# Token factors laid on by VectorE's evictions in an mLSTM and attention layer, with a changed prologue and gate block order

## The chip, the cores and the metric

The kernel runs on one core of a Trainium2 chip. The metric is the device time of one execution in microseconds; the kernel before takes 1875.45 us, the median of 3 runs (1875.11 to 1876.63). All times inside a profile count from the start of the span, and L-numbers are lines of the kernel before.

## What is computed

One decoder layer on x of 1024 tokens by 1024 features, all in float32:

```python
xn   = rms_norm(x, norm_mix_w)
proj = xn @ w_in        # da_q, da_k, da_v, ml_q, ml_k, ml_v, ml_i, ml_f, ml_o, gate_pre
oa   = diff_attention(rope(da_q), rope(da_k), da_v)       # 8 heads, q and k 2 x 64 wide, v 128
qk   = silu(causal_dwconv([ml_q, ml_k]))                  # 4 taps along the tokens
hm   = mlstm_chunkwise(qk[:512], qk[512:], ml_v, ml_i, ml_f)   # 8 heads
ob   = sigmoid(ml_o) * rms_norm(hm)
merged = sigmoid(gate_a) * (oa_normed @ w_proj_a) + sigmoid(gate_b) * (ob @ w_proj_b)
h    = x + merged @ w_out
h    = h + relu(rms_norm(h) @ w_ff1)**2 @ w_ff2
out  = rms_norm(h)
```

The root of the mean square of a token, by which `xn` divides, is one factor for each token. It commutes with the projection, so a projected row may be multiplied by it afterwards. Only that is used in what follows.

## The kernel before, in words

Each engine has its own instruction stream, written out by hand, and waits on semaphores; instructions of one engine run in order.

**Products.** Every float32 product is made of three on TensorE: each operand is split into a high part (a copy of ScalarE into a narrower type, `r1h`, `w_hi`) and a low part (the difference, `r1l`, `w_lo`, by VectorE or GpSimd). A weight block is 128 columns of the projection; a unit is one block for half of the tokens, 24 matmuls of 512 columns into one of the banks `gp[0]`, `gp[1]`. A unit is evicted to `ev[half]` and SP stores it in `proj_d`. `gp_free` counts evictions; TensorE waits before a unit for all but the latest one (L901).

**Blocks.** A head has HB = 6 blocks, 12 units: q (k = 0, 1), k (2, 3), the two values as token units (4 to 7, evicted with a factor of `rstd` for each token), the mLSTM's k and q (8, 9), and the output gate (10, 11). All of a head's units are evicted by ScalarE (`evac`, L1311). The rows of q and k get the token factors with cosT and sinT, which were multiplied by `roots` (L1849, L1850). The rows of blocks 4 and 5 are loaded back as `ckq` and `osig` and multiplied by `roots` on VectorE (L1965, L1978). After the heads come 16 gate blocks, whose units VectorE evicts with a product by `roots` (`gate_evac`, L1877).

**Rounds.** The units of head h+1 run beside the attention and mLSTM of head h (`attend`), in a round of 16 slots. QUARTERS says how many quarters of units TensorE makes in each slot: unit 8 in slot 10, unit 9 in 11, unit 10 in 12 and 13, unit 11 in 14. In a slot TensorE makes its quarters first and then its part of `attend`. The last head goes beside the gate blocks, 1.5 units a slot.

In a round VectorE ropes k and q in slot 0. In slot s = i + 3 it takes the maxima (`nb`) of score tile i, and after ScalarE's exponentials combines the two maps into `at` (L1953), which TensorE transposes in slot s = i + 4 (L1076) and ScalarE and VectorE split (`ath`, `atl`); the right part of a tile follows in slot i + 5 (`low(i, True)`, L1920). In slots 3 to 6 it also makes the convolution (`kqs`), in slot 14 the norm of the mLSTM output (`nd`), and in slot 15 the product into `osig` after TensorE's transposes (L1110).

**Prologue.** SP loads x in chunks of 2 k (`x_load`), weight block 0 after the second. ScalarE makes `r1h`, VectorE `r1l`. TensorE's `first_half` makes the input and forget gates and block 0, alternating every 4 k. ScalarE then squares eight token tiles (L1336) and takes the root (L1362), VectorE its reciprocal, TensorE spreads it by columns (`x_spread`, L940, after two quarters of unit 2) and ScalarE copies that to `roots`. Then ScalarE goes through the units k of head 0 with `prologue_step(k)` between them: exponential and logarithm for the gates (2), `tk` (7), Sin of the tables (8), `dc` (9). VectorE makes the tables beside it, and with `init_done` releases SP's loads of head 0.

**Order of queues.** SP's `head_round` sends the stores of two units, then a weight load, then the loads for `attend` (`att_loads`, L509; in the second round these come first after units 8 and 9). A weight load waits for the low part of the block two before it. ScalarE's and GpSimd's splits are in the same order.

```python
901:  wait(pe, gp_free, 2 * n + half - 1)
1312: wait(act, st[half], 16 * n)
1313: act.wait_ge(gemm_done, 2 * n + half + 1)
1398: for k in range(2 * HB):
1403:     evac(k // 2, k % 2, k - 4 if k // 2 in (2, 3) else None)
1404:     prologue_step(k)
```

Of the kernel before, what the change touches and what calls it, by code (L numbers as in the profile page):

```python
# [19 lines left out]
ALU = mybir.AluOpType  # L20
# [8 lines left out]
NH = 8  # L29
# [147 lines left out]
def build(nc, x, x_rows, x_halves, positions, in_blocks, in_if, columns, da_lambda,  # L177
# [12 lines left out]
    with ExitStack() as ctx:  # L190
# [230 lines left out]
        x_bc, roots_ready, o_scaled = sem("x_roots_spread"), sem("roots_ready"), sem("o_scaled")  # L421
# [39 lines left out]
        DVE_HEAD = 40  # L461
# [5 lines left out]
        def _(sp):  # L467
# [87 lines left out]
            sp.dma_start(wif[:].rearrange("p k n -> p (k n)"), in_if).then_inc(wif_in, 16)  # L555
            x_load(0, 1)
            wload_head(0, 0)
# [335 lines left out]
        def _(pe):  # L893
# [49 lines left out]
            def first_half(i):  # L943

                t = slice(i * HALF, (i + 1) * HALF)
                for part in range(2):
                    ks = range(4 * part, 4 * part + 4)
# [7 lines left out]
                    if part:  # L955
                        gates.then_inc(pro_pe, 1)
# [339 lines left out]
        def _(act):  # L1296
# [47 lines left out]
            for c in range(XC):  # L1344
# [7 lines left out]
                if c == 1:  # L1352
                    split_hi(0, 0, 0)
# [5 lines left out]
            for t in range(TT):  # L1359
                token_square(t)  # L1360
            act.wait_ge(x_sq, TT)
# [8 lines left out]
            def prologue_step(k):  # L1370
# [17 lines left out]
                if k == 8:  # L1388
# [4 lines left out]
                if k == 9:  # L1393
# [4 lines left out]
            for k in range(2 * HB):  # L1398
# [4 lines left out]
                evac(k // 2, k % 2, k - 4 if k // 2 in (2, 3) else None)  # L1403
                prologue_step(k)

            def attend(h, s, evac_units, splits=None, behind_k=None):
# [51 lines left out]
                if s == 7:  # L1458
                    act.wait_ge(conv_done, h + 1)
                    act.activation(sg[:], kqs[:], ACT.Sigmoid).then_inc(sg_ready, 1)  # L1460
                    act.wait_ge(o_scaled, h + 1)
# [28 lines left out]
            def head_round(h, att):  # L1490
                for s in range(SLOTS):
# [6 lines left out]
                    for k in ENDS_AT[s][:-1]:  # L1498
                        evac(h * HB + k // 2, k % 2, k - 4 if k // 2 in (2, 3) else None)

                    def evac_units():
                        for k in ENDS_AT[s][-1:]:
                            evac(h * HB + k // 2, k % 2, k - 4 if k // 2 in (2, 3) else None)
# [264 lines left out]
        def _(dve):  # L1768
# [18 lines left out]
            for i in range(2):  # L1787
                if i:
                    dve.wait_ge(x_in[XC], X_LOADED[XC])
                for k in range(KT):  # L1790
                    x_low(i, k)
                    if i == 0 and k == 3:
                        dve.wait_ge(w_hi, 1)
                        dve.tensor_tensor(wl[0][:], raw[0][:], wh[0][:].bitcast(F32), ALU.subtract).then_inc(w_split, 1)

# [51 lines left out]
            pro.link(dve.tensor_scalar(aw[:], aw[:], 1.0 - LAMBDA_INIT, None, ALU.mult))  # L1847
            dve.wait_ge(pro_act, 7)
            pro.link(dve.tensor_tensor(cosT[:], cosT[:], roots[:], ALU.mult))  # L1849
            pro.link(dve.tensor_tensor(sinT[:], sinT[:], roots[:], ALU.mult))  # L1850
            dve.wait_ge(c2_in, 16 * 2)
            dve.wait_ge(uw_st, 32)
            dve.sem_inc(init_done, 2)

# [22 lines left out]
            def gate_evac(k):  # L1877

                n, half = N_GATE + k // 2, k % 2
                dve.wait_ge(st[half], 16 * n)  # L1880
                dve.wait_ge(gemm_done, 2 * n + half + 1)
                if k == 0:
                    dve.wait_ge(gp_free, 2 * N_GATE)
# [757 lines left out]
```

## Time and profile before

| | |
|---|---|
| median of 3 runs | 1875.45 us (1875.11 to 1876.63) |
| profiled execution | 1879.1 us |
| its span | 1877.3 us, 26794 instructions |
| TensorE busy | 1848.6 us, 98% |
| VectorE, ScalarE, GpSimd busy | 1312.6, 972.0, 318.7 us |
| mean granted clock of TensorE | 0.995 of full |

The page is read from the top: the busy time of each engine shows which one can bound the kernel. Idle time of that engine is then looked up in its waits, where a row names the waiting engine, its tile and line, the releaser, and the sum, number and longest of the waits. A timeline row has start and duration in us, engine, line, operation, tiles and shapes; in brackets stands the idle time before it and what ended it. PEld is TensorE's weight load, SPq an issue on SP's queue.

### The profile page before, as it was taken

How to read it: one execution, taken by the hardware profiler on the slowest of the kernel's cores; microseconds unless marked ns; L12 is line 12 of the kernel's file. 1: busy time of each engine (PE TensorE's matmuls, PEld its weight loads, DVE VectorE, ACT ScalarE, POOL GpSimd, SP SyncE). 2: the span in 40 equal slices, each digit the busy share in tenths (PEclk: the TensorE clock that was granted, in tenths of full speed). 3: DMA queues.
4: the chain of work that ended last, by engine and by line, in shares of the span. 5: the costliest groups of instructions: out<-in, count | busy, mean ns of one | idle time of the engine just before them, and what ended most of it. 6: DMA issues, size and time to landing. Idle time of an engine off the chain costs nothing.

```text
span 1877.3 us, 26794 instructions
## 1 busy us (share of the span) xinstructions
PE 1848.6 (98%) x9698; PEld 1585.2 (84%) x9698; DVE 1312.6 (70%) x1705; ACT 972.0 (52%) x1565; POOL 318.7 (17%) x189
## 2 busy tenths in 40 slices
PE   8999999999999999999999999999999999999998
PEld 6989898989898989888878887878888888888887
DVE  6575858586767767666436867687868778688774
ACT  6355655656565656534214553237676585333343
POOL 2102020211111121244420313520000000021002
PEclk9999999999999999999999999999999999999999
DMA  7342515151424242365457735647768587464412
GB/s 284 96 159 69 179 57 196 50 188 60 159 79 162 84 162 89 133 208 183 146 211 266 257 110 195 219 161 265 243 228 294 192 280 264 157 232 150 154 71 90
DMA packets 112594, 318.34 MB, mean 170 GB/s; under 512 B 11496, under 2 KB 28520, under 8 KB 99456
## 3 DMA queue, kind: packets, MB, share of 16 engines
q1 hardware_dynamic: 110208, 308.86, 47.1%
q10 hardware_dynamic: 2304, 8.39, 1.1%
q8 instruction: 52, 0.85, 0.2%
q14 instruction: 30, 0.25, 0.0%
HBM read 221.71 MB, written 95.49 MB: 169 GB/s over the span
## 4 chain that ended last, share of the span: by engine, by line
PE 85%; DVE 8%; issue 3%; ACT 2%; DMA 1%; SPq 1%; DVEq 0%; POOL 0%; ACTq 0%
PE gp L904 7%; PE gp L906 7%; PE gp L905 7%; PE scores L1206 6%; PE scores L1210 6%; PE scores L1208 6%; PE gp L922 3%; PE gp L924 3%; PE gp L923 3%; PE gp L1206 2%; PE gp L1210 2%; PE gp L1208 2%; PE ob L1062 2%; PE ob L1063 2%; PE scores L1015 2%
## 5 line engine op out<-in xcount | busy, mean ns | idle before, releaser
L904 PE MATMUL gp<-r1h,w_hi 128*128 128x512 f32 x752 | 299.0, 398 | 7.6 <-ACT ev L1320 5.3
L906 PE MATMUL gp<-r1h,w_lo 128*128 128x512 f32 x752 | 295.7, 393 | 0.0
L905 PE MATMUL gp<-r1l,w_hi 128*128 128x512 f32 x752 | 294.8, 392 | 0.0
L1206 PE MATMUL scores<-fxh,fqh 128*128 128x512 f32 x512 | 199.8, 390 | 1.8 <-DVE fxl L2226 1.7
L1210 PE MATMUL scores<-fxh,fql 128*128 128x512 f32 x512 | 199.2, 389 | 0.0
L1208 PE MATMUL scores<-fxl,fqh 128*128 128x512 f32 x512 | 199.2, 389 | 0.0
L904 PEld LDWEIGHTS gp<-r1h,w_hi 128*128 128x128 f32 x752 | 142.4, 189 | 37.1 <-issue 3.4
L906 PEld LDWEIGHTS gp<-r1h,w_lo 128*128 128x128 f32 x752 | 142.1, 189 | 30.6
L905 PEld LDWEIGHTS gp<-r1l,w_hi 128*128 128x128 f32 x752 | 142.4, 189 | 27.8
L2452 POOL TENSOR_TENSOR w_lo<-w_raw,w_hi 128x1024 fp32r<-128x1024 f32 x25 | 60.5, 2421 | 501.7 <-ACT w_hi L1309 486.6
L924 PE MATMUL gp<-w_hi_pair,r1l 128*128 128x256 f32 x512 | 144.8, 283 | 0.0
L922 PE MATMUL gp<-w_hi_pair,r1h 128*128 128x256 f32 x512 | 144.8, 283 | 0.0
L923 PE MATMUL gp<-w_lo_pair,r1h 128*128 128x256 f32 x512 | 144.8, 283 | 0.0
L1449 ACT ACTIVATE pr<-scores,nb 128x256 f32<-128x256 f32 (+7 forms) x128 | 94.2, 739 | 77.3 <-DVE nb L1940 76.7
L2233 DVE TENSOR_TENSOR fxl<-xraw,fxh 128x2048 fp32r<-128x2048 f32 x54 | 123.3, 2283 | 0.0
L1629 ACT ACTIVATE fqh<-rq 128x2048 fp32r<-128x2048 f32 x32 | 61.2, 1913 | 106.2 <-DVE rq L2262 65.2
L1206 PEld LDWEIGHTS scores<-fxh,fqh 128*128 128x128 f32 x512 | 96.1, 188 | 22.6 <-DVE fxl L2226 2.1
L1208 PEld LDWEIGHTS scores<-fxl,fqh 128*128 128x128 f32 x512 | 96.1, 188 | 20.1 <-issue 0.2
L1210 PEld LDWEIGHTS scores<-fxh,fql 128*128 128x128 f32 x512 | 96.1, 188 | 20.0
L1641 ACT ACTIVATE fxh<-xraw 128x2048 fp32r<-128x2048 f32 x54 | 102.7, 1902 | 6.1 <-DMA xraw<-xo_d 6.1
L2237 DVE TENSOR_TENSOR fql<-rq,fqh 128x2048 fp32r<-128x2048 f32 x32 | 73.2, 2287 | 43.0 <-ACT fqh L1629 43.0
L923 PEld LDWEIGHTS gp<-w_lo_pair,r1h 128*128 128x128 f32 x512 | 97.4, 190 | 0.4
(426 smaller groups left out, 4536.2 us busy)
## 6 DMA issues: line engine op xcount, KB each, us to landing
xraw<-xo_d SPq DMA_DIRECT2D x62, 1024.0 KB, 4.8
w_raw<-in_in_blocks SPq DMA_DIRECT2D x64, 512.0 KB, 3.7
proj_d<-ev SPq DMA_DIRECT2D x128, 256.0 KB, 2.3
rq<-in_ff_quarters SPq DMA_DIRECT2D x32, 1024.0 KB, 7.6
xo_d<-res SPq DMA_DIRECT2D x78, 256.0 KB, 3.3
xo_d<-ring SPq DMA_DIRECT2D x60, 256.0 KB, 3.2
xo_d<-item SPq DMA_DIRECT2D x24, 256.0 KB, 2.5
pq<-in_sq_quarters SPq DMA_DIRECT2D x5, 1024.0 KB, 7.1
```

What stands on the lines that cost most here:

```text
L904: pe.matmul(gp[half][:], wh[slot][:, k, :], hi[:, k, t], start=(k == 0), stop=False)
L905: pe.matmul(gp[half][:], wh[slot][:, k, :], lo[:, k, t], start=False, stop=False)
L906: mm = pe.matmul(gp[half][:], wl[slot][:, k, :], hi[:, k, t], start=False, stop=(k == KT - 1))
L922: pe.matmul(to, r1h[:, kk, t], whp[:, kk].rearrange("p a n -> p (a n)"), start=(kk == 0), stop=False)
L923: pe.matmul(to, r1h[:, kk, t], wlp[:, kk].rearrange("p a n -> p (a n)"), start=False, stop=False)
L924: mm = pe.matmul(to, r1l[:, kk, t], whp[:, kk].rearrange("p a n -> p (a n)"), start=False, stop=(kk == KT - 1))
L1206: pe.matmul(bank, qh[s % 3][:, k, cols], xh[s % 3][:, k, :], start=first and k == 0, stop=False, skip_group_check=True)
L1208: pe.matmul(bank, qh[s % 3][:, k, cols], xl[s % 3][:, k, :], start=False, stop=False, skip_group_check=True)
L1210: mm = pe.matmul(bank, ql[s % 3][:, k, cols], xh[s % 3][:, k, :], start=False, stop=(k == UN - 1), skip_group_check=True)
L1449: act.activation(pr[:, c, 0:(i + 1) * P], sp_[:, c, 0:(i + 1) * P], ACT.Exp, bias=nb[:, c:c + 1], scale=-1.0, accum_out=rs[:, i, c:c + 1]) ...
L1641: act.activation(xh[s % 3][:], xraw[(s + 1) % 2][:], ACT.Copy).then_inc(p_hi, 1)
L2233: dve.tensor_tensor(xl[s % 3][:], xraw[(s + 1) % 2][:], xh[s % 3][:].bitcast(F32), ALU.subtract).then_inc(p_lo, 1)
```

## The change

It has six parts.

1. `scaled_evac` on VectorE evicts a unit with a product by `roots`; `head_evac` uses it for units 8 to 11 of every head, and `gate_evac` for the gate blocks. ScalarE skips these units. Where the evicting engine changes, the later one waits for the earlier one's count (k == 8 on VectorE, k == 0 on ScalarE).
2. The products by `roots` on `ckq` and `osig` are gone, with the semaphore `o_scaled`.
3. In a round `head_evac` stands before VectorE's part of `attend`, in slot 14 behind it. In the last round the gate evictions of slot 14 stand behind `attend` too.
4. In the prologue SP issues weight block 0 before the second chunk of x; ScalarE splits it after the first chunk and VectorE after two `r1l`; TensorE alternates every 2 k.
5. ScalarE evicts unit 0 behind the second token square.
6. Sin stands at step 7 of the prologue and `dc` at step 8. VectorE evicts units 8 to 11 of head 0 around the products of cosT and sinT, units 10 and 11 after it has signalled `init_done`.

```diff
             x_load(0, 0)
             sp.dma_start(cols[:], columns).then_inc(cols_in, 16)
             sp.dma_start(wif[:].rearrange("p k n -> p (k n)"), in_if).then_inc(wif_in, 16)
+            wload_head(0, 0)
             x_load(0, 1)
-            wload_head(0, 0)
...
-                for part in range(2):
-                    ks = range(4 * part, 4 * part + 4)
+                for part in range(4):
+                    ks = range(2 * part, 2 * part + 2)
...
                 x_high(0, 2 * c + 1)
-                if c == 1:
+                if c == 0:
                     split_hi(0, 0, 0)
...
             for t in range(TT):
                 token_square(t)
+                if t == 1:
+                    evac(0, 0)
...
-                if k == 8:
 
                     for i, tab in enumerate((sinT, cosT)):
...
-                if k == 9:
+                if k == 8:
                     act.wait_ge(pro_pe, 4)
...
-                evac(k // 2, k % 2, k - 4 if k // 2 in (2, 3) else None)
+                if 0 < k < 8:
+                    evac(k // 2, k % 2, k - 4 if k // 2 in (2, 3) else None)
...
-                    act.wait_ge(o_scaled, h + 1)
+                    act.wait_ge(o_in, 16 * h + 16)
...
                     def evac_units():
                         for k in ENDS_AT[s][-1:]:
-                            evac(h * HB + k // 2, k % 2, k - 4 if k // 2 in (2, 3) else None)
+                            if k == 0:
+                                act.wait_ge(gp_free, 2 * (h * HB))
+                            if k < 8:
+                                evac(h * HB + k // 2, k % 2, k - 4 if k // 2 in (2, 3) else None)
...
                     x_low(i, k)
-                    if i == 0 and k == 3:
+                    if i == 0 and k == 1:
...
+            def scaled_evac(n, half, behind=None):
+
+                dve.wait_ge(st[half], 16 * n)
+                dve.wait_ge(gemm_done, 2 * n + half + 1)
+                if behind is not None:
+                    dve.wait_ge(gp_free, behind)
+                dve.tensor_tensor(ev[half][:], gp[half][:], roots[:, half * HALF:(half + 1) * HALF], ALU.mult).then_inc(gp_free, 1)
+                dve.wait_ge(gp_free, 2 * n + half + 1)
+                dve.sem_inc(ev_ready[half], 1)
+
+            def head_evac(h, k):
+
+                n = h * HB + k // 2
+                scaled_evac(n, k % 2, 2 * n if k == 8 else None)
...
+            head_evac(0, 8)
             dve.wait_ge(pro_act, 7)
             pro.link(dve.tensor_tensor(cosT[:], cosT[:], roots[:], ALU.mult))
             pro.link(dve.tensor_tensor(sinT[:], sinT[:], roots[:], ALU.mult))
+            head_evac(0, 9)
             dve.wait_ge(c2_in, 16 * 2)
             dve.wait_ge(uw_st, 32)
             dve.sem_inc(init_done, 2)
+            head_evac(0, 10)
+            head_evac(0, 11)
...
+            def attend_round(h, s):
+
+                ends = [k for k in ENDS_AT[s] if k >= 8]
+                if s == SLOTS - 2:
+                    attend(h, s)
+                for k in ends:
+                    head_evac(h + 1, k)
+                if s != SLOTS - 2:
+                    attend(h, s)
...
-                    chain.link(dve.tensor_tensor(ckq[:, CONV - 1:], ckq[:, CONV - 1:], roots[:], ALU.mult))
...
-                        dve.wait_ge(o_in, 16 * h + 16)
-                        dve.tensor_tensor(osig[:], osig[:], roots[:], ALU.mult).then_inc(o_scaled, 1)
...
             for s in range(SLOTS):
+                if s == SLOTS - 2:
+                    attend(NH - 1, s, lows=False)
                 for k in GATE_UNITS_AT[s]:
                     if k > 2:
                         gate_evac(k)
-                attend(NH - 1, s, lows=False)
+                if s != SLOTS - 2:
+                    attend(NH - 1, s, lows=False)
```

## Rows read from the trace of the kernel before

**Rows 1.** The page, part 1: busy time, share of the span, instructions.

```profile
PE 1848.6 (98%) x9698; PEld 1585.2 (84%) x9698; DVE 1312.6 (70%) x1705; ACT 972.0 (52%) x1565; POOL 318.7 (17%) x189
```

**Rows 2.** Waits of TensorE: sum, number, longest, in us.

```profile
PE tr L1076 <- DVE at L1953: 7.2, 7, 1.1
PE gp L904 <- ACT ev L1320: 5.3, 2, 3.0
...
PE gp L904 <- POOL w_lo L2446: 2.3, 1, 2.3
```

**Rows 3.** Windows: one microsecond after the first stop of TensorE.

```profile
35.00:36.00 1.00, 1.00 (x4) 0.81 (x3) 0.00 (x0) 0.95 (x2) 0.37 (x1) 0.50 0.97 367
```

**Rows 4.** Timeline of the first 12 us, SP, ScalarE and TensorE.

```profile
2.13 0.43 SPq L550 DMA_DIRECT2D xt<-in_x_halves  x1
...
2.60 0.43 SPq L479 DMA_DIRECT2D w_raw<-in_in_blocks  x1
...
6.83 1.33 ACT L1340 ACTIVATE r1h<-xt,cols 128x512 fp32r<-128x512 f32 x2 [0.37 <-DMA xt<-in_x_halves]
...
8.88 1.06 ACT L1301 ACTIVATE w_hi<-w_raw 128x1024 fp32r<-128x1024 f32 x1 [0.71 <-DMA w_raw<-in_in_blocks]
...
11.25 0.19 PEld L960 LDWEIGHTS gp<-r1h,w_hi 128*128 128x128 f32 x1 [0.43 <-DVE w_lo L1794]
```

**Rows 5.** Timeline of ScalarE at the end of the token squares.

```profile
32.87 0.30 ACT L1362 ACTIVATE rstd<-ss,eps 128x8 f32<-128x8 f32 x1
33.08 1.30 ACT L1320 ACTIVATE ev<-gp 128x512 f32<-128x512 f32 x2
```

**Rows 6.** Timeline of TensorE around its first stop.

```profile
30.42 0.39 PE L962 MATMUL gp<-r1h,w_lo 128*128 128x512 f32 x1
33.80 0.47 PE L904 MATMUL gp<-r1h,w_hi 128*128 128x512 f32 x1 [2.99 <-ACT ev L1320]
...
38.21 1.05 PE L940 MATMUL tr<-ident,rstd 128*128 128x128 f32 x8
```

**Rows 7.** Timelines of VectorE, SP and ScalarE, 84 to 113 us.

```profile
84.61 1.23 DVE L1849 TENSOR_TENSOR cosT<-cosT,roots 128x1024 f32<-128x1024 f32 x1 [13.85 <-ACT dc L1395]
85.87 3.30 DVE L1850 TENSOR_TENSOR sinT<-sinT,roots 128x1024 f32<-128x1024 f32 x1
...
89.29 0.34 SPq L517 DMA_DIRECT2D kraw<-proj_d  x1
...
94.68 1.56 SPq L495 DMA_DIRECT2D proj_d<-ev  x2
...
102.48 0.60 ACT L1320 ACTIVATE ev<-gp 128x512 f32<-128x512 f32 x1 [4.68 <-DMA proj_d<-ev]
...
112.33 0.58 ACT L1320 ACTIVATE ev<-gp 128x512 f32<-128x512 f32 x1
```

**Rows 8.** Two lines of VectorE: min, median, max ns of one.

```profile
L1965 DVE TENSOR_TENSOR ckq<-ckq,roots x8: 1217/1219/1219, 120.0 to 825.7; 128x1024 f32<-128x1024 f32 x8
...
L1884 DVE TENSOR_TENSOR ev<-gp,roots x32: 677/691/692, 796.1 to 1001.0; 128x512 f32<-128x512 f32 x32
```

**Rows 9.** Timelines of VectorE and TensorE in slots 3 to 5 of a head.

```profile
317.41 1.22 DVE L1965 TENSOR_TENSOR ckq<-ckq,roots 128x1024 f32<-128x1024 f32 x1
...
322.64 0.44 PE L1076 MATMUL tr<-ident,at 128*128 128x128 f32 x2 [1.13 <-DVE at L1953]
```

**Rows 10.** Timeline of VectorE in slot 10.

```profile
361.45 0.42 DVE L1920 TENSOR_TENSOR atl<-tr,ath 128x256 fp32r<-128x256 f32 x1 [0.72 <-ACT ath L1426]
```

**Rows 11.** Timelines of VectorE, ScalarE and TensorE, slots 14 and 15 of the last round.

```profile
946.42 0.69 DVE L1884 TENSOR_TENSOR ev<-gp,roots 128x512 f32<-128x512 f32 x1 [4.75 <-PE gp L906]
...
951.97 1.06 ACT L1301 ACTIVATE w_hi<-w_raw 128x1024 fp32r<-128x1024 f32 x1 [0.49 <-PE gp L906]
...
955.50 0.52 PE L904 MATMUL gp<-r1h,w_hi 128*128 128x512 f32 x1 [2.34 <-POOL w_lo L2446]
```

**Rows 12.** Timeline of VectorE in slot 6 of the last round.

```profile
853.86 0.69 DVE L1884 TENSOR_TENSOR ev<-gp,roots 128x512 f32<-128x512 f32 x1 [5.60 <-DMA proj_d<-ev]
```

More of the change, by code:

```diff
@@ L420, in build @@
         x_sq, tok_in, x_std, x_rstd = (sem(n) for n in ("x_squared", "fourth_tokens_in", "x_std", "x_rstd"))
-        x_bc, roots_ready, o_scaled = sem("x_roots_spread"), sem("roots_ready"), sem("o_scaled")
+        x_bc, roots_ready = sem("x_roots_spread"), sem("roots_ready")
         x_hi, x_lo = sem("x_hi"), sem("x_lo")
@@ L459, in build @@
         ft_tr, ft_out, ft_act, out_st = sem("ft_tr"), sem("ft_out"), sem("ft_act"), [sem("out_st0"), sem("out_st1")]
-        DVE_HEAD = 40
+        DVE_HEAD = 39
         block = ctx.enter_context(nc.Block())
@@ L954, in first_half @@
                         gates = pe.matmul(sbank[:, i, :], wifl[:, k, :], r1h[:, k, t], start=False, stop=(k == KT - 1))
-                    if part:
+                    if part == 3:
                         gates.then_inc(pro_pe, 1)
@@ L1498, in head_round @@
                     for k in ENDS_AT[s][:-1]:
-                        evac(h * HB + k // 2, k % 2, k - 4 if k // 2 in (2, 3) else None)
+                        if k < 8:
+                            evac(h * HB + k // 2, k % 2, k - 4 if k // 2 in (2, 3) else None)
                     def evac_units():
                         for k in ENDS_AT[s][-1:]:
-                            evac(h * HB + k // 2, k % 2, k - 4 if k // 2 in (2, 3) else None)
+                            if k == 0:
+                                act.wait_ge(gp_free, 2 * (h * HB))
+                            if k < 8:
+                                evac(h * HB + k // 2, k % 2, k - 4 if k // 2 in (2, 3) else None)
                     attend(att, s, evac_units, splits if s >= 9 else None)
@@ L1877, in gate_evac @@
             def gate_evac(k):
[L1879 to L1883, printed above, removed]
-                dve.tensor_tensor(ev[half][:], gp[half][:], roots[:, half * HALF:(half + 1) * HALF], ALU.mult).then_inc(gp_free, 1)
-                dve.wait_ge(gp_free, 2 * n + half + 1)
-                dve.sem_inc(ev_ready[half], 1)
+                scaled_evac(N_GATE + k // 2, k % 2, None if k else 2 * N_GATE)
+            def attend_round(h, s):
[6 more added lines that the diff above has]
+                    attend(h, s)
             def attend(h, s, lows=True):
@@ L2037, in _ @@
             for s in range(SLOTS):
-                attend(0, s)
+                attend_round(0, s)
             with dve.Fori(1, NH - 1) as h:
                 for s in range(SLOTS):
-                    attend(h, s)
+                    attend_round(h, s)
             for s in range(SLOTS):
+                if s == SLOTS - 2:
+                    attend(NH - 1, s, lows=False)
                 for k in GATE_UNITS_AT[s]:
```

## The prediction

> **What bounds the kernel now.** I read the page first: TensorE is busy for 98% of the span [rows 1]. So only two things can shorten this kernel: fewer products on TensorE, of which the change removes none, or less idle time and less slow clock on it. Next came the waits of TensorE alone [rows 2]: seven waits of some 1.1 us on `at` of VectorE (one in each of seven heads, 7.2 us together), two on an eviction of ScalarE (5.3 us), one on a weight split of GpSimd (2.3 us). Others have no part in the change. Third, the clock [rows 3]: after the long idle stretches the granted clock falls from 2.4 to 1.2 GHz. In the first stretch, until 37.7 us, matmuls start 0.43 us apart in place of 0.228; the twelve from 33.80 to 38.21 [rows 6] take 4.4 us for 12 x 0.228 = 2.7, so the slow stretch costs 1.7. The same follows the idle times of 2.3 us before 112.96 and before 955.50; the idle times of 1.1 us are followed by none. Last, for each wait, the timelines of the other engines, to see who was late and why.
>
> **Start.** SP now issues weight block 0 (at 2.13 us) before the second chunk of x (2.60); ScalarE splits it after the first chunk, VectorE takes its low part after two `r1l`, and TensorE alternates gates and block every 2 k instead of 4. Today the second chunk, issued at 2.13, is there at 6.8, and block 0, issued at 2.60, at 8.9 [rows 4]. If the two landings swap, the high part is ready at 6.85 + 1.06 = 7.9, the low part at 7.95 + 1.22 = 9.2, and TensorE, after its first six gate products, asks for it at about 9.7. The second chunk at 8.9 gives `r1l` of k=2 at 10.3; TensorE wants it at 11.1. No wait is left, and the one on the split [rows 4], with the slow first matmul behind it, goes: 0.25 us. Bounds: nothing gained if the landings keep their times in other order, and a loss (third rival).
>
> **First eviction.** Today both evictions of block 0 stand behind eight token squares and the root, at 33.08 us, though the half-0 unit was done at 19.8. TensorE stops at 30.8 and goes on at 33.80 [rows 5, 6]. The change puts `evac(0, 0)` behind the second square, at about 25.2. It pushes six squares and the root by 0.6 + 0.1: the root lands at 33.9, its reciprocal on VectorE at 34.2. TensorE now begins unit 2 at 30.65, does 12 products (2.75 us), and at 33.4 meets the next late thing, the reciprocal that `x_spread` reads: 0.85 us idle, less than the 1.1 that leaves the clock up. `x_spread` (1.7) and 12 more products end at 38.75; today they end at 39.92 + 2.73 = 42.65. Gain 3.9, of which I take 3.8. Bound below: with the slow clock after 0.85 us all the same, 2.1.
>
> **Second wait on an eviction (110.6 to 112.96).** Its chain [rows 7]: `dc` and the two tables arrive late (Sin stands at step 8, `dc` at step 9), so cosT and sinT are multiplied at 84.61 to 89.2; that releases the loads of head 0 (89.29); SP issues twelve of them and a weight load before the store of unit 10 (94.68), which needs some 7.7 us; ScalarE waits for it until 102.48, then makes seven copies in order, and its next eviction is at 112.33. The change moves Sin to step 7 and `dc` to step 8 and leaves units 8 to 11 to VectorE. With the clock of the first term (TensorE 3.9 earlier): Sin ends near 73.2, the split of block 5 moves behind it (ScalarE 74.2, GpSimd 76.7, wanted by TensorE at 79), `dc` at 74.5, the two table products end by 77.1, or by 79.2 if they stretch as `sinT` did. VectorE then waits for unit 9 (79.4), evicts it, and releases the loads at 80.3, about 4.9 us earlier against TensorE than today. The store of unit 10 goes out near 86 and has 9 us. What VectorE now has in front of its rope work: the evictions of units 10 and 11, so that this begins at 91.1, 1.3 us later against TensorE. ScalarE evicts (head 1, unit 0) when TensorE has made it (95.9), reads `kraw` at 96.6 (roped at 94.9), and its next eviction ends at 106.4; TensorE wants it at 106.8. The wait of 2.29 and its slow stretch of 1.7 go: 4.0. The margin is 0.4 us.
> Here a rule can be weighed. The two table products ran 1.23 and 3.30 us [rows 7], the second beside a GpSimd split of 2.40. The Trainium skill, SBUF — State Buffer, section Who interferes with whom, says that a VectorE instruction with two SBUF inputs and a GpSimd one that reads SBUF exclude each other for a whole instruction. The trace agrees. By the rule the products, now beside the split of block 5, end at 79.2, without it at 77.1; both are before unit 9 is done, so the term is 4.0 by either, and only the chance of the second rival is larger with it.
>
> **Heads.** Removed for each head: `ckq` x `roots` and `osig` x `roots`, 1.22 us each, eight times [rows 8], on VectorE. Added: four evictions of 0.69 us on VectorE [rows 8]; removed: four of some 0.6 on ScalarE. VectorE's sum rises by 4 x 0.69 - 2.44 = 0.3 us a head, but the place counts. The product on `ckq` (317.41) stands between `at` of tile 0 and `at` of tile 1, and TensorE idles 1.13 us for the latter, from 321.5 [rows 9]. Without it all that follows on VectorE comes at least 1.22 earlier: `at` ends at 321.3. That leaves 0.1 to 0.2 us of margin. What is late next is nothing in this round with an idle row. The evictions stand where VectorE waits on TensorE anyway: units 8 and 9 at the head of slots 10 and 11, before `low(i, second)`. Added waits: on `gemm_done`, on the store of the buffer, and once a head on ScalarE's eviction of unit 7. For slot 10: `at` ends at 360.73, unit 7 is evicted at 360.86, the new one runs to 361.65, and `atl` ends at 362.1 instead of 361.87; TensorE asks for it at 362.64 [rows 10]. Unit 10 falls into free time in slot 13; unit 11 delays `osig` by 0.15 us in slot 15, which 0.5 us of idle before `ka` absorbs. Cover of 0.5 us, then; if it is gone, each of the four costs TensorE up to 0.69. Term: of 7.2 us I take 6.9. Bounds: 0 and 7.2.
>
> **Last round.** In slot 14 VectorE waits for units 21 and 22 before it starts on `nd` of the last head, though ScalarE had brought that at 935.7. So `nd` is done at 952.0, ScalarE stands behind its root until 950.1, splits the next weight at 951.97, GpSimd its low part until 955.45, and TensorE idles 0.32 and 2.34 us, with 1.7 of slow clock [rows 11]. With `attend` first, `nd` takes 935.8 to 940.5, before unit 21 is done (940.9), the split follows at 941 and GpSimd's at 944.5; TensorE wants it at 952.7. Gain 0.3 + 2.3 + 1.7 = 4.3. What is late next is nothing: the front's first loads wait for the store of `ob` as before and are wanted 20 us later.
>
> **Sum.** 0.25 + 3.8 + 4.0 + 6.9 + 4.3 = 19.2 us of 1879.1, the profiled execution (span 1877.3 and 1.8 around it): 1859.9. The median of the timed runs is 3.65 below that execution; with the same terms it becomes 1875.45 - 19.2 = 1856.2.
>
> **Rivals.**
> 1. The heads keep their wait: the chain from the eviction of unit 0 to `at` of tile 1 is tight, the margin 0.1 us, and one more late item in slot 5, 10 or 11 takes it back. For: the margins; against: every duration in that chain repeats within 0.01 us. Gain 12 to 13, 1863.
> 2. The wait at 110.6 stays, since VectorE's queue now holds two evictions before its rope work and the margin is 0.4 us. Gain 15.2, 1860.2.
> 3. Block 0 still lands at 8.9 or later: TensorE then stops at 9.7 for the low part until 11.3 (8.9 + 1.06 + 1.22), 1.6 us, with ScalarE's second chunk queued behind the split, and perhaps a slow stretch of 1.7. Gain 15.6 to 17.5, about 1859. The Trainium skill, DMA: Bandwidth & Descriptors, section Queues, rings and completion order, says that transfers issued in order need not complete in order; the landings here came in order of issue.
> 4. Slower: in slot 10 VectorE waits for the store of unit 6 before it may evict unit 8, and `low` and all of slot 10 stand behind it. One such wait of 5.6 us is in the trace, in the last round [rows 12], where TensorE did not stop. Beyond 0.8 us of cover TensorE would idle 4.8 us and get 1.7 of slow clock, 6.5 x 7 heads = 45, net 26 slower: 1902. It decides from 3.5 us of wait per head on. Against: in the round that I read, the store of unit 6 is issued at 349.6, 11 us ahead.
> 5. The idle time goes, but comes back at a later point that does not move, so that nothing is seen: 1875. Against: no wait behind 1000 us hangs on the start.
>
> **How the numbers follow.** Forecast 0.60 (1853 to 1859 by its own bounds), rival 1: 0.15, rival 2: 0.09, rival 3: 0.07, rival 4: 0.04, rival 5: 0.03, mixtures of the first three 0.02. Low end 1852.5: all terms full, a further wait of 0.9 us in the last head gone, and some 3 us for the distance between profiled and timed runs. High end 1865: rival 1, or 2 and 3 together. A change of 0.2% (3.75 us) is what a measurement of this kernel can tell; all of the first four cases are beyond it. Faster 0.93, same 0.03, slower 0.04.
>
> **What would show it.** Waits of TensorE: no row `tr <- at` of 1.1 us; no row on ScalarE's `ev` of 3.0 or 2.3; none on GpSimd's `w_lo` of 2.3; a new one before `tr<-ident,rstd` of under 1 us. The granted clock is full from 7 us until the turn near 1150. TensorE's time per head round falls from 98.8 to 97.7 us. `kraw` of head 0 is loaded at about 81. I am wrong if TensorE waits for `atl` or a `gp` bank in slots 5 or 10 to 14, if VectorE waits for a store there, or if a half-rate stretch appears before 38 us.

## The result, and the profile after

The kernel after takes 1857.61 us, the median of 4 runs (1856.95 to 1859.87), against 1876.04 for the kernel before (4 runs): a ratio of 0.9898, 95% interval 0.9883 to 0.9912. The profiled execution took 1859.87 us, its span is 1858.1; that is 19.2 us less than the profiled execution of before. The forecast was 19.2 less, 1859.9 for a profiled execution and 1856.2 for the median. Line numbers of after differ from those of before: L1808 is VectorE's `scaled_evac`, L1981 writes `at`, L1948 `atl`, L2218 `res`.

The page, part 1, to be held against [rows 1]:

```profile
PE 1843.9 (99%) x9698; PEld 1581.4 (85%) x9698; DVE 1314.7 (71%) x1721; ACT 952.7 (51%) x1533; POOL 317.8 (17%) x189
```

TensorE has the same 9698 matmuls, 4.7 us less busy time (less of it at 1.2 GHz) and 14.5 us less outside it. The waits of TensorE say which idle time went, against [rows 2]:

```profile
PE scores L931 <- POOL wifl L2483: 2.6, 1, 2.6
PE gp L1168 <- DVE res L2218: 2.2, 1, 2.2
PE scores L1206 <- DVE fxl L2254: 1.7, 1, 1.7
PE ob L1062 <- DVE atl L1948: 0.9, 1, 0.9
PE gp L904 <- DVE ev L1808: 0.5, 1, 0.5
```

All seven waits on `at`, both on ScalarE's `ev` and the one on `w_lo` are gone; one of 0.5 us on VectorE's eviction is new. A sum of waits does not show the clock, though. So I paired every matmul of after with its partner in before and followed the difference of their starts. It changes at few places:

| place (time in before) | difference before and behind it | in the forecast |
|---|---|---|
| start, up to unit 2 (30.65) | 0 to +0.27 | -0.25 |
| first eviction (30.8 to 37.4) | +0.27 to -4.42 | -3.8 |
| second wait on an eviction (112.96 to 117) | -4.33 to -8.33 | -4.0 |
| heads, seven waits on `at` | -8.33 to -15.64 | -6.9 |
| gate unit 3 (805.87) | -15.64 to -15.14 | none |
| last round (952 to 959) | -15.14 to -19.80 | -4.3 |
| front and rest | -19.80 to -19.26 | none |

A negative difference means that after is ahead. The last row is no part of the change as far as the runs show: the half microsecond arises between 960 and 1100 us, and in the run start_undone below, whose code is the same as after's there, the difference stays at -19.78 to -19.79.

**First eviction.** The timelines of ScalarE, VectorE and TensorE of after around 24 to 36 us, against [rows 5, 6]:

```profile
24.57 0.58 ACT L1320 ACTIVATE ev<-gp 128x512 f32<-128x512 f32 x1
...
33.21 0.30 ACT L1364 ACTIVATE rstd<-ss,eps 128x8 f32<-128x8 f32 x1
...
33.54 0.20 DVE L1839 RECIPROCAL rstd<-rstd 128x8 f32<-128x8 f32 x1
...
33.42 0.39 PE L906 MATMUL gp<-r1h,w_lo 128*128 128x512 f32 x1
33.80 1.16 PE L940 MATMUL tr<-ident,rstd 128*128 128x128 f32 x8
...
35.61 0.47 PE L904 MATMUL gp<-r1h,w_hi 128*128 128x512 f32 x1
```

TensorE's last product of the first half of unit 2 starts at 33.42 and the spread of the roots at 33.80: nearly no stop, where I had 0.85 us. I had the eviction push the root by 0.7 us, so that it would end at 33.9; it ends at 33.51, 0.34 later than in before (33.17). In after ScalarE stands idle for 0.89 us ahead of the sixth square, which waits for its tokens, and part of the eviction's time falls into that.

**Second wait.** Timelines of VectorE, SP, ScalarE and TensorE, against [rows 7]:

```profile
74.48 2.95 DVE L1871 TENSOR_TENSOR cosT<-cosT,roots 128x1024 f32<-128x1024 f32 x1
77.47 1.22 DVE L1872 TENSOR_TENSOR sinT<-sinT,roots 128x1024 f32<-128x1024 f32 x1
...
80.51 0.35 SPq L517 DMA_DIRECT2D kraw<-proj_d  x1
...
85.94 0.77 SPq L495 DMA_DIRECT2D proj_d<-ev  x1
...
95.59 0.60 ACT L1320 ACTIVATE ev<-gp 128x512 f32<-128x512 f32 x1 [2.89 <-PE gp L906]
...
105.46 0.58 ACT L1320 ACTIVATE ev<-gp 128x512 f32<-128x512 f32 x1
...
106.18 0.40 PE L904 MATMUL gp<-r1h,w_hi 128*128 128x512 f32 x1
```

Each link lies where the forecast put it within 1 us: loads at 80.5 (80.3), the store of unit 10 at 85.9 (86), ScalarE's eviction at 95.6, the next one's end at 106.04 (106.4), 0.14 us ahead of TensorE's 106.18. Of the two table products the one that runs beside GpSimd's split takes 2.95 us, the other 1.22. In the run steps_undone below the split is over by 73.28 and they take 1.23 and 1.22. The splits, first of after, then of steps_undone:

```profile
73.95 2.40 POOL L2480 TENSOR_TENSOR w_lo<-w_raw,w_hi 128x1024 fp32r<-128x1024 f32 x1 [13.32 <-ACT w_hi L1309]
```

```profile
70.88 2.40 POOL L2481 TENSOR_TENSOR w_lo<-w_raw,w_hi 128x1024 fp32r<-128x1024 f32 x1 [10.57 <-ACT w_hi L1309]
```

So the rule weighed in the forecast (the Trainium skill, SBUF — State Buffer, Who interferes with whom) agrees with the trace, and it decided nothing, as both orders end before unit 9 is done.

**Heads.** Timelines of VectorE and TensorE in slot 5, against [rows 9]:

```profile
310.88 0.48 DVE L1981 SCALAR_TENSOR_TENSOR at<-pr,cc 128x256 f32<-128x256 f32 x1
...
311.32 0.28 PE L1063 MATMUL ob<-vs,atl 128*128 128x256 f32 x1
311.44 0.42 PE L1076 MATMUL tr<-ident,at 128*128 128x128 f32 x2
```

`at` is there at 311.36 and TensorE takes it at 311.44: a margin of 0.08 us.

### The profile page after: what moved, and what is told of

It is laid out like the page before. It is cut to its first block, busy times and chain, and to the rows that moved or that the text cites. A ratio compares the mean times of both kernels' runs of the same rounds, so it can differ in the third digit from the quotient of the medians.

```text
span 1858.1 us, 26783 instructions
## 1 busy us (share of the span) xinstructions
PE 1843.9 (99%) x9698; PEld 1581.4 (85%) x9698; DVE 1314.7 (71%) x1721; ACT 952.7 (51%) x1533; POOL 317.8 (17%) x189
## 4 chain that ended last, share of the span: by engine, by line
PE 95%; DVE 3%; issue 1%; ACT 0%; DMA 0%; POOL 0%; DVEq 0%; ACTq 0%; POOLq 0%
PE gp L904 9%; PE gp L906 9%; PE gp L905 9%; PE scores L1206 6%; PE scores L1208 6%; PE scores L1210 6%; PE gp L922 3%; PE gp L924 3%; PE gp L923 3%; PE gp L1206 2%; PE gp L1210 2%; PE gp L1208 2%; PE ob L1062 2%; PE scores L1015 2%; PE scores L1014 2%; PE ob L1063 2%
## 5 line engine op out<-in xcount | busy, mean ns | idle before, releaser
L1635 ACT ACTIVATE fqh<-rq 128x2048 fp32r<-128x2048 f32 x32 | 61.2, 1913 | 106.4 <-DVE rq L2290 65.3
L1808 DVE TENSOR_TENSOR ev<-gp,roots 128x512 f32<-128x512 f32 x64 | 44.0, 688 | 90.9 <-PE gp L906 75.8
```

## The experiments

Each run was timed beside the kernel before on the same chip; its median there is given. Differences of a few tenths are read from pairs of matmuls, as above, not from medians.

### One part alone: the last round

```diff
             for s in range(SLOTS):
+                if s == SLOTS - 2:
+                    attend(NH - 1, s, lows=False)
                 for k in GATE_UNITS_AT[s]:
...
-                attend(NH - 1, s, lows=False)
+                if s != SLOTS - 2:
+                    attend(NH - 1, s, lows=False)
```

> The kernel before with one part of the change: in slot 14 of the last round VectorE's gate evictions stand behind its part of attend. By my step for the last round TensorE's idle times of 0.32 us (on nd) and 2.34 us (on GpSimd's w_lo) and the slow stretch behind them (1.7) go: 4.3 us less than before, some 1871.7; the traces of before and after, laid on each other, show 4.7 there. Rival: the split's lateness is only handed on to the next weight block, and the wait comes back one block later; then within 1 us of before. Second rival: the clock falls at that place whatever the idle time; then 2.7 less.

Measured: 1872.74 against 1877.34, ratio 0.9971 (0.9959 to 0.9983). The difference of starts goes from +0.60 to -4.10 between 952 and 959 us: 4.7, of which 0.32 and 2.34 are the two waits and 2.0 the slow clock with the restart behind it. The term stands; I had that part 0.3 too low. The row that was late, TensorE's wait on `w_lo` [rows 2], has no successor.

### One part alone: the first eviction

```diff
             for t in range(TT):
                 token_square(t)
+                if t == 1:
+                    evac(0, 0)
...
-                evac(k // 2, k % 2, k - 4 if k // 2 in (2, 3) else None)
+                if k > 0:
+                    evac(k // 2, k % 2, k - 4 if k // 2 in (2, 3) else None)
```

> The kernel before with one part of the change: ScalarE evicts unit 0 behind the second token square. By my step: the stop of 2.99 us at 33.80 is replaced by one of 0.85 us at the spread of the roots and the slow stretch of 1.7 goes, 3.8 us less in the first 45 us. Traces of before and after laid on each other show 4.7 between 30 and 45 us, as that new wait is only 0.15 there. What this leaves open is the second wait on an eviction (2.29 us at 112.96): if it is paced by ScalarE's own chain from the start, it moves with TensorE and stays 2.3; if it hangs on something that did not move (the loads of the tables), it grows by up to what was gained and the whole is 0 to 2 us less. Rival: a gain of only 2.1, with a half-rate stretch behind the short wait.

Measured: 1872.69 against 1877.34, ratio 0.9973 (0.9963 to 0.9984). In the profiled execution the difference is -4.80 at 37.4 us and -4.91 up to the second wait. What is left of the waits on `ev`, 5.3 us in two before:

```profile
PE gp L904 <- ACT ev L1320: 1.7, 1, 1.7
```

The second wait on an eviction did not grow. Its chain moved with TensorE (and half a microsecond more), as the sum of the forecast needs. But it did not stay as it was either: this stop, of 1.73 us where before has 2.29, had no half-rate stretch behind it, and the difference goes on to -6.9 and stands at -6.5 from the first wait on `at` on. In this execution the early eviction alone gave 1.6 us of what the forecast counts under the second wait. The median is 4.65 below that of before.

### Which product makes `at` late

```diff
-                    chain.link(dve.tensor_tensor(ckq[:, CONV - 1:], ckq[:, CONV - 1:], roots[:], ALU.mult))
```

> The kernel before without one instruction a head, the product of ckq by the roots (the convolution then works on rows without their token factors). The product on osig and ScalarE's evictions stay. By my step for the heads this product alone makes at of tile 1 late: the seven waits of TensorE on at (7.2 us) go to nothing or a few hundredths, 6.9 to 7.3 less than before, 1868.3. Rival: the waits come from the whole load on VectorE (both products) or from ScalarE's eviction of unit 0 ahead of the high part; then half of it or less goes, over 1871.

Measured: 1867.82 against 1877.34, ratio 0.9949 (0.9934 to 0.9965). No wait on `at` is left, and the period of a head falls from 98.81 to 97.51 us: 1.30 for a wait of 1.1. The 0.2 on top has no row of its own. TensorE's timelines of before, then of no_ckq_product, show it:

```profile
321.22 0.28 PE L1063 MATMUL ob<-vs,atl 128*128 128x256 f32 x1
322.64 0.44 PE L1076 MATMUL tr<-ident,at 128*128 128x128 f32 x2 [1.13 <-DVE at L1953]
```

```profile
321.23 0.28 PE L1063 MATMUL ob<-vs,atl 128*128 128x256 f32 x1
321.35 0.38 PE L1076 MATMUL tr<-ident,at 128*128 128x128 f32 x2
```

From start to start 1.42 us become 0.12, a difference of 1.30. The row says 1.13 because it counts from the end of a matmul of 0.28 us, behind whose start the next one would come after 0.12. One product of 1.22 us, on an engine that is 70% busy, accounts for all of the heads' term. The median fell by 9.5 us, more than the 6.9 to 7.3 expected (the interval reaches from 6.6 to 12.4); in the profiled execution the heads give 8.3, from +1.76 at 117 us to -6.55 at 780.

The counter-test puts that product back into the kernel after:

```diff
                     dve.wait_ge(kq_in, 16 * h + 16)
+                    chain.link(dve.tensor_tensor(ckq[:, CONV - 1:], ckq[:, CONV - 1:], roots[:], ALU.mult))
```

> The kernel after with the product of ckq by the roots put back ahead of the convolution (the factor is then on twice). By my step VectorE's at of tile 1 is late again by 1.22 us less the margin of 0.1, so seven or eight waits of some 1.1 us: 7 to 8.5 us more than after, 1865 to 1866. Rival: the change has moved other work out of that chain (ScalarE's evictions of units 8 to 11), so that the product is covered: within 1 us of after, 1857.6.

Measured: 1866.72 us, ratio to before 0.9946 (0.9932 to 0.996), so 9.1 over after's median, a little above the range expected. The waits of TensorE have the old row again:

```profile
PE tr L1076 <- DVE at L1981: 7.9, 7, 1.2
```

Its head period is 99.06, after's 97.70: 1.36 a head, 9.5 for seven. And 99.06 is 0.25 more than before's 98.81, with the same product in the same place. So the change costs the heads something too. The trace of the kernel without the product and that of after, laid on each other, show where. Timelines of ScalarE and TensorE, first of after, then of no_ckq_product, at unit 3 of a head:

```profile
594.13 0.58 ACT L1320 ACTIVATE ev<-gp 128x512 f32<-128x512 f32 x1
...
594.76 0.50 PE L904 MATMUL gp<-r1h,w_hi 128*128 128x512 f32 x1
595.11 0.40 PE L905 MATMUL gp<-r1l,w_hi 128*128 128x512 f32 x1
```

```profile
603.38 0.58 ACT L1320 ACTIVATE ev<-gp 128x512 f32<-128x512 f32 x1
...
604.19 0.39 PE L904 MATMUL gp<-r1h,w_hi 128*128 128x512 f32 x1
604.41 0.39 PE L905 MATMUL gp<-r1l,w_hi 128*128 128x512 f32 x1
```

In after the eviction of unit 1 ends at 594.71 and TensorE starts at 594.76, with 0.35 to the next matmul in place of 0.22: 0.18 us late, a wait too short to be listed. VectorE's timelines, of after and of no_ckq_product, show where that comes from:

```profile
577.68 0.69 DVE L1808 TENSOR_TENSOR ev<-gp,roots 128x512 f32<-128x512 f32 x1 [0.52 <-PE gp L906]
578.71 0.75 DVE L2058 SCALAR_TENSOR_TENSOR osig<-tr,hw,osig 128x512 f32<-128x512 f32 x1 [0.34 <-PE ob L1110]
```

```profile
587.62 0.75 DVE L2032 SCALAR_TENSOR_TENSOR osig<-tr,hw,osig 128x512 f32<-128x512 f32 x1 [0.94 <-PE tr L1110]
```

The two traces are 9.43 us apart at this point, so `osig` comes 0.52 us later in after, behind the eviction of unit 11. The idle time ahead of `ka` takes up 0.33 of it (0.46 becomes 0.13), and the rest reaches ScalarE's eviction of unit 1. No run moves unit 11 alone, so that this eviction is the cause is read from the traces.

### Is that short wait worth anything?

ScalarE evicts unit 1 ahead of its copy of `v` in slot 0:

```diff
+                    if early:
+                        early()
                     act.wait_ge(v_in, 16 * h + 16)
...
-                            if k < 8:
+                            if k < 8 and k != 1:
...
-                    attend(att, s, evac_units, splits if s >= 9 else None)
+                    attend(att, s, evac_units, splits if s >= 9 else None, None, (lambda: evac(h * HB, 1)) if s == 0 else None)
```

> The kernel after with one move: in slot 0 of a round ScalarE evicts unit 1 of the next head ahead of its copy of v. Traces of the kernel without the ckq product and of after, laid on each other, show TensorE 0.18 us later once a head, at unit 3, where the eviction of unit 1 ends at 594.71 and TensorE's matmul starts at 594.76, too short to have a row among the waits. If that eviction is the cause, 7 x 0.18 = 1.2 us less than after, 1856.3. Rival: the step is only a slower matmul with no wait in it; then no change, or a wait on vs in its place.

Measured: 1857.63 us, nothing gained. The wait at unit 3 did go (the difference to after falls by 0.2 there, in each head), and comes back within 10 us, at the transposes of `at`; the period is 97.69. With a margin of 0.08 us at `at`, that is the next limit. So that the eviction of unit 1 made TensorE late was right, the gain was not.

### The second wait: which part ends it

The order of the steps undone in after:

```diff
-                if k == 8:
+                if k == 9:
                     act.wait_ge(pro_pe, 4)
...
+                if k == 8:
                     for i, tab in enumerate((sinT, cosT)):
```

> The kernel after with Sin of the tables back at step 8 and dc back at step 9 of the prologue; all else as after. By my step for the second wait the move is what brings the tables, so the loads of head 0 and the store of unit 10 forward: with Sin behind the split of block 5 and the eviction of unit 7, cosT and sinT are multiplied some 5 us later, VectorE's evictions of units 9 to 11 and the rope work stand behind them, and TensorE waits again near 106 to 110, by 1 to 3 us, with a slow stretch if the wait is over 2: 1 to 5 us more than after. Rival: the evictions by VectorE have taken away the chain that made it (ScalarE waiting for the store of unit 10), and the order of Sin and dc is worth nothing: within 0.5 us of after.

Measured: 1857.39 us, no difference. The timelines of ScalarE and VectorE say why:

```profile
72.11 1.06 ACT L1394 ACTIVATE sinT<-sinT 128x1024 f32<-128x1024 f32 x1
...
74.03 0.20 ACT L1397 ACTIVATE dc<-scores 128x64 f32<-128x64 f32 x1
```

```profile
74.58 1.23 DVE L1872 TENSOR_TENSOR cosT<-cosT,roots 128x1024 f32<-128x1024 f32 x1
75.84 1.22 DVE L1873 TENSOR_TENSOR sinT<-sinT,roots 128x1024 f32<-128x1024 f32 x1
```

Sin starts at 72.11, in after at 70.92: one split later and no more. In before the evictions of units 8 and 9 stood between these steps, as its ScalarE shows:

```profile
79.85 1.06 ACT L1392 ACTIVATE sinT<-sinT 128x1024 f32<-128x1024 f32 x1
...
83.57 0.60 ACT L1320 ACTIVATE ev<-gp 128x512 f32<-128x512 f32 x1 [1.71 <-PE gp L906]
84.29 0.22 ACT L1395 ACTIVATE dc<-scores 128x64 f32<-128x64 f32 x1
```

With ScalarE free of them, steps 8 and 9 follow at once. The run does not undo what it meant to undo. The other half of the question is the steps moved in the kernel before, where ScalarE still evicts everything:

```diff
-                if k == 8:
-
                     for i, tab in enumerate((sinT, cosT)):
...
-                if k == 9:
+                if k == 8:
                     act.wait_ge(pro_pe, 4)
```

> The kernel before with one part of the change: Sin of the tables at step 7 and dc at step 8, ScalarE still evicting all units of head 0. By my step for the second wait, earlier tables bring the loads of head 0 and so the store of unit 10 forward by some 5 us, ScalarE no longer waits for it, and TensorE's stop of 2.3 us at 113 goes with its slow stretch: 3.5 to 4.0 less than before. Rival, from the run steps_undone: it is ScalarE's leaving units 8 to 11 to VectorE that ends the wait, because dc then has no eviction ahead of it; here dc stands behind the eviction of unit 8, which is made at 75 to 79 us, so the loads come only some 2 to 3 us earlier and the stop stays or shrinks by less than 1 us.

Measured: 1873.74 against 1876.89, ratio 0.9983 (0.9975 to 0.9992). The difference of starts goes from +0.80 to -3.08 at 113 us, 3.9. SP loads `kraw` at 85.51 and stores unit 10 at once behind the loads; ScalarE evicts without a wait for the store:

```profile
100.69 0.60 ACT L1320 ACTIVATE ev<-gp 128x512 f32<-128x512 f32 x1 [2.10 <-PE gp L906]
...
110.54 0.58 ACT L1320 ACTIVATE ev<-gp 128x512 f32<-128x512 f32 x1
```

So the forecast's chain holds by itself, and in after the evictions on VectorE are enough without the steps: of these two parts the change needs one. Whether the evictions would be enough without the early eviction of unit 0 was not tried. My rival, that the stop stays here, was wrong.

### The start

In after the old order is restored (start_undone); in before the new one is put in (start_only):

```diff
+            wload_head(0, 0)
             x_load(0, 1)
-            wload_head(0, 0)
...
-                for part in range(2):
-                    ks = range(4 * part, 4 * part + 4)
+                for part in range(4):
+                    ks = range(2 * part, 2 * part + 2)
...
```

> The kernel after with the order of the start undone: second chunk of x before weight block 0, high part after the second chunk, low part after four r1l, TensorE alternating every 4 k. By my step the wait on the split comes back with its slow first matmul, 0.25 us more than after. The profile of after showed TensorE 0.27 us later at unit 2 than before, 0.35 of it already there at the first gate product. If that is the start order's doing, this kernel is 0.3 us faster than after; if it is only a difference between one execution and another, the first product's time differs from run to run and has nothing to do with the order.

Measured: 1857.52 us, no difference; the first gate product of this execution starts at 8.54 us, with the old order. So the +0.27 of the table is not shown to be part of the change: over 14 profiled executions that product starts between 7.17 and 8.69 us, with either order.

> The kernel before with one part of the change: the order of the start (weight block 0 before the second chunk of x, its splits earlier, TensorE alternating every 2 k). By my step: 0.25 us less than before. By the five profiled executions with this order so far, TensorE waits for the low part of block 0 for 0 (twice), 0.35, 1.09 and 1.76 us, once with a slow stretch behind it, as the block's landing varies; by that the profiled execution is 0 to 3 us later at the first stop, but the eviction that ends this stop hangs on the token squares and not on TensorE, so the total changes by less than 0.5 us in either direction.

Measured: 1876.76 against 1876.89, ratio 0.9996 (0.9985 to 1.0008): nothing. The split of block 0 starts at 6.69 to 8.62 us in seven executions with the new order and at 8.06 to 9.38 in seven with the old. The block lands about 1.2 us earlier, and is wanted earlier too; TensorE waits for its low part for 1.76, 1.09 and 0.35 us in three of the seven. With the old order it waits for it for 0.42 and 0.31 us in two of seven. What follows hides it: the stop or the spread of the roots ends with the root, which starts between 32.6 and 34.2 us in all of them.

### The place of the evictions

```diff
-                if s == SLOTS - 2:
-                    attend(h, s)
+                attend(h, s)
                 for k in ends:
                     head_evac(h + 1, k)
-                if s != SLOTS - 2:
-                    attend(h, s)
```

> The kernel after with head_evac behind attend in every slot, as in slot 14. By my step placement ahead of attend costs nothing (cover of 0.5 us in slot 10), and behind it the bank comes free up to 10 us later while TensorE needs it one unit (5.5 us) later: if the unit's successor in the same bank is due first, TensorE waits in slots 12 and 15 or at the next unit 0, 1 to 3 us a head, 7 to 20 us more than after. Rival: attend's part in those slots is done before TensorE asks, and the place is worth nothing: within 1 us of after.

Measured: 1857.8 us, nothing; the head period is 97.70 as in after. In slot 10 `atl` now comes ahead of the eviction and nobody waited for either. My price of 7 to 20 us supposed that TensorE would ask for the bank before `attend` was through; it never did.

### Four more moves of this kind

The rows of after show stops that the change left. The kernel three_more moves four things: gate unit 1 is evicted ahead of the roped sum of q, in slot 9 of the last round the eviction stands behind the right `low`, the first `wo_sum` stands ahead of the last four `m_low`, and `x_lo_part(0)` ahead of `scaled(6, 1)`.

```diff
+                        if not lows and x_ is qraw:
+                            gate_evac(1)
                         dve.tensor_tensor(x_[:], x_[:], turned[:], ALU.add).then_inc(roped, 1)
...
                         low(i, True)
+                    if not lows and s == 9:
+                        for k in GATE_UNITS_AT[s]:
+                            gate_evac(k)
...
-                        pe.wait_ge(m_lo, 4 * UN)
-                for k in range(KT):
+                        pe.wait_ge(m_lo, 3 * UN)
+                ks = (4, 5, 6, 7, 0, 1, 2, 3) if no == 2 else range(KT)
+                for k in ks:
+                    if no == 2 and k == 0:
+                        pe.wait_ge(m_lo, 4 * UN)
...
             wo_sum(0, 0)
+            for u in range(UN):
+                m_low(C12, u)
             wo_sum(1, 0)
...
             q_lo_part(0)
-            scaled(6, 1)
             x_lo_part(0)
+            scaled(6, 1)
```

> The kernel after with four more moves of the same kind, each read from a row of its profile: in the last round gate unit 1 is evicted before the long roped sum of q (wait of 0.49 us at 790.73), in slot 9 the eviction stands behind the right low part of at (0.86 at 869.38), the first sum of the output projection stands before the last four low parts, with TensorE beginning the third unit with k = 4 to 7 (2.22 at 1147.11, and a slow stretch of some 1.6), and the low part of x stands before scaled(6, 1) (0.65 of 1.72 at 1228.63). All together 5.8 us less than after, 1851.8. Rival: each wait is handed on to the next late item; the sum is then under 2.

Measured: 1854.12 us, ratio to before 0.9881 (0.9865 to 0.9898), 3.5 under after. Against after the difference of starts falls by 0.65, 0.98 and 4.1 at the first three places, as expected; the fourth gives 0.67 and loses 0.68, to a wait of 0.52 on `sqacc` 13 us later. The profiled execution also shows the start at its worst. Timelines of ScalarE and TensorE:

```profile
8.62 1.06 ACT L1304 ACTIVATE w_hi<-w_raw 128x1024 fp32r<-128x1024 f32 x1 [1.47 <-DMA w_raw<-in_in_blocks]
```

```profile
10.99 0.50 PE L960 MATMUL gp<-r1h,w_hi 128*128 128x512 f32 x1 [1.76 <-DVE w_lo L1803]
...
12.50 0.60 PE L952 MATMUL scores<-r1h,wifh 128*128 128x512 f32 x1
12.90 0.63 PE L953 MATMUL scores<-r1l,wifh 128*128 128x512 f32 x1
13.33 0.63 PE L954 MATMUL scores<-r1h,wifl 128*128 128x512 f32 x1
```

That is the forecast's third rival, as priced there: a wait for the low part, and a half-rate stretch behind it (matmuls up to 0.43 us from start to start). TensorE is 2.65 us behind after at unit 2, which is past the root, so that here it counts.

The last kernel leaves out the fourth move, takes back the order of the start and adds unit1_early:

> The kernel three_more without its fourth move (scaled(6, 1), whose 0.67 us came back as a wait of 0.52 on sqacc some 13 us later), with the old order of the start (no wait of 1.76 us on w_lo and no slow stretch at 12.5 us), and with unit 1's eviction ahead of the copy of v. From start_undone (1857.5): 0.65 at 790, 0.98 at 870, 1.7 at the output projection (2.2 and a slow stretch in those executions that have one), 1.2 from the heads: 4.5 less, 1853.0. Rival: waits handed on, not under 1855.

Measured: 1853.97 us (1853.42 to 1854.6), ratio to before 0.988 (0.9866 to 0.9894); unit1_early took 1857.63 on the same chip, so 3.7 less. Against start_undone the steps are 0.65, 0.99 and 1.74, and nothing from the heads. The expected 1.2 for these was unit1_early's, and wrong for the same reason.

## Why the prediction was right, point by point

- **Sum and size.** Right: 19.2 forecast, 19.2 between the profiled executions, 18.4 between the medians (1857.61 where I had 1856.2). That the two agree to a tenth is luck. The first eviction came out 0.9 us larger than forecast and the heads and the last round 0.4 each; the start, gate unit 3 and the front took 0.5 us each that no term had. The signs named ahead came: no row on ScalarE's `ev` or on `w_lo` of GpSimd, full clock from 7.6 to 1147.7 us, 97.70 us a head, `kraw` loaded at 80.5. Only the short stop at the spread is missing.
- **Start.** Wrong, though small. The step took the landings of one execution as fixed. They spread by 2 us, the order as such is worth nothing in either kernel, and the place hangs on the root behind it. The third rival, with a chance of 0.07, showed its wait in three of seven executions, once with the half-rate stretch.
- **First eviction.** Right in mechanism, too low: 4.7 for 3.8. The stop of 0.85 us was nearly none in after (0.53 and 0.65 in moved_five and ckq_back). The step that failed is that the eviction pushes all squares behind it by its full length: the root ends at 33.51, not 33.9. And since the spread hangs on the root, the 0.27 that TensorE was late at the start came back here: 0.7 of the 0.9 are these two. The root's own time differs by 1.6 us between executions, though (it starts at 32.61 in evac0_only, which has the early eviction, and at 32.87 in before), so 0.4 us is less than one trace can tell.
- **Second wait.** Right, 4.0 for 4.0, and the chain link by link. Not seen: with the rest of the change in place, the evictions on VectorE would have done it without the steps.
- **Heads.** Right, 7.3 for 6.9, and the cause is shown from both sides. Two small things were missed, and they work against each other: each wait costs 0.2 us more than its row says, and some 0.2 a head goes back because unit 11's eviction delays slot 0. The forecast had a delay of 0.15 us in slot 15, absorbed by 0.5 us of idle; it is 0.52, and 0.33 of it were absorbed.
- **Last round.** Right, 4.7 for 4.3. Missed: VectorE's eviction of gate unit 1 now binds TensorE by 0.49 us at 790.73, part of the same delay. In before that eviction ended at 805.81, just ahead of TensorE's matmul at 805.87.
- **Profiled run and median.** The forecast carried the distance of 3.65 us over without a cause. The runs point to one. At the stop of the output projection TensorE waits 1.61 to 1.78 us in seven profiled executions, none with a half-rate stretch, and 2.22 to 2.25 in five, four of them with one. Both profiled executions, before and after, are of the second kind; start_undone differs from after at this place by 2.2 us. The four with the stretch took 2.3 to 4.7 us more than the medians of their kernels, the other eight between 2.3 less and 0.5 more. For after that covers the whole distance (2.26 us); for before some 1.4 of the 3.65 stay open, and executions without a trace can't be looked into.

The windows view of one microsecond behind that stop, of after and then of start_undone (busy time and number of PE, PEld, VectorE, ScalarE and GpSimd; last three columns: granted clock, DMA share, GB/s):

```profile
1148.00:1149.00 1.00, 1.00 (x4) 0.77 (x3) 0.00 (x0) 0.00 (x0) 0.00 (x0) 0.50 0.85 279
```

```profile
1146.50:1147.50 1.00, 1.00 (x6) 0.82 (x5) 0.26 (x1) 0.08 (x1) 0.00 (x0) 1.00 0.93 160
```

Four matmuls in a microsecond at 1.2 GHz, six at 2.4.

## What to carry to other kernels

Where the bounding engine is 98% busy and keeps its work, what is left to gain lies in a handful of waits; find for each the one instruction that makes it late, and see whether it can stand elsewhere or go. Price a wait by the starts before and behind it and not by its row, which was 0.2 us short here, and add the half-rate stretch: it followed 17 of the 18 stops of 2.2 us and more between products in these traces and cost up to 2.0 us. A gain at one place is only kept as far as the next margin: 0.08 us here made a correct fix of 0.2 us a head worth nothing, and a gain hidden by a slower chain (the root) was none at all.

## What the runs showed of the hardware

- The length of an idle time alone does not say whether TensorE's clock falls. Of stops of 1.6 to 1.8 us behind products, more than ten were followed by full clock, but the one of 1.76 us at 10.99 in three_more by 3.4 us at 1.2 GHz from 12.5 us on; the one of 1.93 us at 114.97 in no_ckq_product had a half-rate stretch, and of five stops of 2.2 us at the output projection one had none. All of 2.29 us and more behind the first products had one. Why these differ was not tried.
- The same load of weight block 0, issued at 2.13 us, is split by ScalarE from 6.69 to 8.62 us in seven executions, 0.02 us behind its landing each time, and the first gate product of TensorE starts between 7.17 and 8.69 in fourteen. Steps of under a microsecond in the first 12 us can't be read from one profile.
